# HGRN2 and retention heads: output matmuls behind the first eighth of the next head's first tile, back-transposes behind its seventh

## What is computed

```python
def _layer(x, c, pos, state, lb, g_norm, w_ada, b_ada, w_in, conv_w, conv_b, b_i, b_f, skip, w_gn, w_out):
    mod = jax.nn.silu(c) @ w_ada + b_ada
    shift, scale, gate = jnp.split(mod, 3, axis=-1)
    h = _rmsnorm(x, g_norm) * (1.0 + scale[:, None, :]) + shift[:, None, :]
    cols = jnp.split(h @ w_in, np.cumsum(COL_SIZES)[:-1].tolist(), axis=-1)
    hq, hf, hi, mq, mk, mv, mi, mf, rq, rk, rv, z = cols
    ...
    o = jnp.concatenate([
        _head_norm(o_hg, w_gn[:W_HG], False),
        _head_norm(o_ml, w_gn[W_HG:W_HG + W_ML], True) + skip * q_c.astype(jnp.float32),
        _head_norm(o_rt, w_gn[W_HG + W_ML:], True)], axis=-1)
    o = o.astype(x.dtype) * jax.nn.silu(z)
    y = x + gate[:, None, :] * (o @ w_out)
```

```python
        inter = inter_d[None, :, :, None] * jnp.einsum('bhtk,bhkv->bhtv', qc, s)
        sc = jnp.einsum('bhtk,bhsk->bhts', qc, kc) * intra_d[None]
        intra = jnp.einsum('bhts,bhsv->bhtv', sc, vc)
        s_new = (chunk_d[None, :, None, None] * s
                 + jnp.einsum('bhsk,bhsv->bhkv', kc * state_d[None, :, :, None], vc))
        return s_new, inter + intra
```

## Time and profile before

| what | us |
|---|---|
| median of 3 runs (2352.44 to 2353.47) | 2353.13 |
| span of the profiled execution | 2351.4 |
| TensorE matmuls busy, of this span | 2296.5 |
| VectorE busy | 1283.2 |
| ScalarE busy | 753.7 |
| GpSimd busy | 938.6 |

### The profile page before, as it was taken

One profiled execution on the slowest core, in us unless ns is written; L12 is line 12 of the kernel. 1 busy time (PEld: TensorE's weight loads), 2 busy tenths in 40 slices (PEclk: granted clock), 3 DMA queues, 4 the chain that ended last, 5 costly groups with the idle time before them and its releaser, 6 DMA issues.

```text
span 2351.4 us, 50350 instructions
## 1 busy us (share of the span) xinstructions
PE 2296.5 (98%) x21251; PEld 2174.7 (92%) x21251; DVE 1283.2 (55%) x2499; ACT 753.7 (32%) x1219; POOL 938.6 (40%) x668
## 2 busy tenths in 40 slices
PE   5899999999999999999999999999999999999998
PEld 3799999999999999998888999999999999999998
DVE  5465666677776333442127566567767744345444
ACT  2243332333333333421114333233333333334111
POOL 2143343444333444453333333343333344346552
PEclk8999999999999999999999999999999999999999
DMA  9972333555554434368887233355554434433443
GB/s 365 352 230 76 92 92 109 156 155 155 155 155 123 114 102 110 101 194 257 247 283 215 74 92 92 92 155 155 156 158 106 125 98 109 116 95 109 109 120 107
DMA packets 473482, 347.22 MB, mean 148 GB/s; under 512 B 18701, under 2 KB 417513, under 8 KB 471937
## 3 DMA queue, kind: packets, MB, share of 16 engines
q1 hardware_dynamic: 473258, 344.02, 49.9%
HBM read 312.07 MB, written 32.09 MB: 146 GB/s over the span
## 4 chain that ended last, share of the span: by engine, by line
PE 90%; DVE 4%; DMA 3%; DVEq 1%; issue 1%; ACT 1%; POOL 1%; SPq 0%; ACTq 0%; POOLq 0%
PE pj L722 72%; PE mx L728 3%; DMA rows<-in_w_ada 2%; PE mx L1087 2%; PE mx L1113 2%; PE mx L843 1%; PE mx L1101 1%; PE mx L809 1%; PE pj L1220 1%; PE mx L1065 1%; PE mx L1115 1%; PE mx L1105 1%; DVE t L1598 1%; PE mx L990 1%; DMA rows<-in_x_prompt 1%
## 5 line engine op out<-in xcount | busy, mean ns | idle before, releaser
L722 PE MATMUL pj<-hh,whi 128*128 128x260 f32 x4928 | 1419.9, 288 | 7.9 <-DVE hl L1598 7.6
L690 POOL TENSOR_TENSOR wlo<-raw,whi 128x512 fp32r<-128x512 f32 x632 | 893.0, 1444 | 1311.7 <-ACT whi L1302 1311.7
L722 PE MATMUL pj<-hl,whi 128*128 128x260 f32 x4928 | 1393.3, 283 | 0.0
L722 PE MATMUL pj<-hh,wlo 128*128 128x260 f32 x4928 | 1390.7, 282 | 0.0
L722 PEld LDWEIGHTS pj<-hh,whi 128*128 128x128 f32 x4928 | 929.4, 189 | 52.5 <-issue 47.1
L722 PEld LDWEIGHTS pj<-hl,whi 128*128 128x128 f32 x4928 | 929.1, 189 | 0.0
L722 PEld LDWEIGHTS pj<-hh,wlo 128*128 128x128 f32 x4928 | 928.6, 188 | 0.0
L1302 ACT ACTIVATE whi<-raw 128x2048 fp32r<-128x2048 f32 x158 | 302.9, 1919 | 252.0 <-PE pj L722 174.2
L1302 ACT ACTIVATE xv<-pj 128x260 f32<-128x260 f32 x188 | 64.7, 383 | 388.0 <-PE pj L722 387.8
L1598 DVE SCALAR_TENSOR_TENSOR o<-pj,mod,t 128x260 f32<-128x260 f32 (+1 forms) x56 | 24.6, 480 | 231.1 <-PE pj L722 215.5
L1302 ACT ACTIVATE t<-t 128x520 f32<-128x520 f32 (+1 forms) x125 | 78.9, 631 | 170.9 <-DVEq L1852 124.3
(11 more groups left out here) (304 smaller groups left out, 2329.8 us busy)
## 6 DMA issues: line engine op xcount, KB each, us to landing
raw<-in_w_in SPq DMA_DIRECT2D x256, 512.0 KB, 5.3
raw<-in_w_out SPq DMA_DIRECT2D x64, 512.0 KB, 5.5
lev<-in_w_ada SPq DMA_DIRECT2D x90, 256.0 KB, 4.9
rows<-in_w_ada SPq DMA_DIRECT2D x22, 1024.0 KB, 12.1
lev<-in_w_ada SPq DMA_DIRECT2D x39, 512.0 KB, 6.0
out<-ss SPq DMA_DIRECT2D x32, 512.0 KB
xv<-in_w_ada SPq DMA_DIRECT2D x25, 512.0 KB, 5.8
y_kept<-o SPq DMA_DIRECT2D x2, 4160.0 KB, 15.9
```

Of the source, the lines that this page charges most:

```text
L690: last = e.tensor_tensor((wlo_third if t == 2 else wlo[:, par, :])[:, cs], w[:, cs], high_of(t)[:, cs].bitcast(F32), ALU.subtract)
L722: last = e.matmul(pj[:, 2 * par + b, 0:HALF], w[:, par, kb * P:(kb + 1) * P], x[:, kb, b * HALF:(b + 1) * HALF], start=(kb == 0 and m == 0 ...
```

## The change

Two hook tables in `hooks_of`, and nothing else. HGRN2 heads (4 per layer) and retention heads other than the very first and the last of a layer (4 in the first layer, 5 in the second) get `outputs` behind part 0 of the next head's tile 0 and `back` behind part 6 of it. These are 17 places. The last head of each layer (h = 15) keeps its table, so do the mLSTM heads and the very first head.

```diff
                         if kind == "hg":
                             own = ({}, {2: (level_scores((-1, 0)),),
                                         **{lv + 2: (level_scores((lv,)),) for lv in range(1, 6)}},
-                                   {0: (level_scores((6,)),), 2: (rows,), 5: (states_u,), 7: (outputs,)})
-                            return own, {5: (back,)}
+                                   {0: (level_scores((6,)),), 2: (rows,), 5: (states_u,)})
+                            return own, {0: (outputs,), 6: (back,)}
...
-                        return ({}, {}, {1: (scores, rows), 5: (states_u,), 7: (outputs,)}), {5: (back,)}
+                        if h + 1 == NH:
+                            return ({}, {}, {1: (scores, rows), 5: (states_u,), 7: (outputs,)}), {5: (back,)}
+                        return ({}, {}, {1: (scores, rows), 5: (states_u,)}), {0: (outputs,), 6: (back,)}
```

## The result

The changed kernel takes 2358.89 us (median of 10 runs, 2356.79 to 2359.59) against 2352.84 us for the kernel before (10 runs, 2352.32 to 2356.22): a ratio of 1.0023 with a 95% interval of 1.0015 to 1.0031, slower by 0.23%. The prediction was 2349.4 us, faster by 0.16%, in a range of 2348.2 to 2351.9. It was wrong in sign and in size, by 9.5 us.

A forecast was written before the change was run, and what follows sets the result against it. TensorE was taken to bound the kernel, running through 90% of the span. Removing its waits at 17 places gains 3.7 us, all other terms 0: 2353.1 - 3.7 = 2349.4 us, range 2348.2 to 2351.9.

The forecast's parts named there:

- What bounds the kernel, and the wait that goes: TensorE bounds the span; its wait for VectorE's `ss` at L1113 goes, weight-load waits falling from 32 to 15.
- (b): At L1113 the switch has a larger step of its own, 0.21 us: gain 2.2 us, time 2350.9 us; chance 0.10.
- (c): At L1113 the 0.31 us step is the instruction's cost, not a wait: nothing gained, 2353.1 us; chance 0.05.
- The size of the gain: At 17 places the step from L722 to L1113 falls to 0.12 us: 5.78 us less 17 x 0.12, 3.74 us.
- the move itself: Instructions of `outputs` take 2.30 us at a tile's edge and inside a tile alike, so the place costs 0.
- rival (a): All of the weight loads' wait at `outputs` comes back: 0.26 us each, 4.4 us for 17 places, 2348.7 us; chance 0.09.
- The tile's wait: Next head's tile 0 needs its low weights 2.6 us sooner; GpSimd's slack hides this, cost 0.
- `back`: TensorE's wait for `ho` at `back` stays 0; VectorE's chain there becomes about 0.9 us shorter.
- Rival (d): At eight HGRN2 places VectorE's chain, held by GpSimd, makes `back` wait 1.33 us each: 2360.0 us; chance 0.04.
- What now runs later: `outputs` starts 1.28 us later against the tiles, as do VectorE's work, `back` and `head_done`; those waiting for them lose 0.
- VectorE goes on to the next head: Tightest case is head 5: its first convolution slips 0.3 us, absorbed by idle time before the next; cost 0.
- a later stretch: Sign of a wrong forecast: the mLSTM heads or the edge between layers take back what the 17 places give.

The follow-up runs named there:

- additions first: The changed kernel with the two 8-column additions of `gate_scans` ahead of its five scans: 2348.49 us against 2353.17 for the kernel before, ratio 0.9979.
- states earlier: The changed kernel, gate-scan additions ahead of the scans, `states_u` behind part 4 instead of 5 in ten mLSTM heads and each layer's last: 2352.42 us against 2352.77.
- `outputs` alone: The changed kernel with `back` behind part 5 again in all 17 places, only `outputs` moved: 2348.68 us against 2352.77 for the kernel before, ratio 0.9983.

## Why the prediction was wrong

**What bounds the kernel, and the wait that goes: right.** All 17 steps fell from at least 0.31 to 0.12 us, and the weight loads' waits for `ss` from 32 to 15, the number written down. Rivals (b) and (c) have fallen with that.

**The size of the gain: too small.** I had 3.74 us. The offset between the traces of additions first and of before, without the start-up and the edge between the layers, is 5.25 us over the 17 places. The term "the move itself" was put at 0, by the very first head, where `outputs` takes 2.30 us, as at the edge. In the moved places it takes 2.20 us. The very first head is a poor witness, because it waits too. It is one of the 32 in the earlier trace rows, and its step is 0.30 us like the others', with `ss` ending at 154.75:

```profile
154.53 0.28 PE L722 MATMUL pj<-hl,whi 128*128 128x260 f32 x1
...
153.53 1.22 DVE L1592 TENSOR_TENSOR ss<-ss,mx 128x1024 f32<-128x1024 f32 x1 [0.17 <-issue]
```

Behind a wait the second L1113 starts 0.21 us after the first, behind none 0.11, which is why the first four are busy for 0.71 us in the earlier trace rows and for 0.61 in the moved places. The mLSTM heads of the kernel states earlier show the same: in each of the ten whose `states_u` is moved, the 2.40 us of the kernel before became 2.30 as the step fell from 0.32 or 0.33 to 0.12. So the 0.10 us belongs to the wait and goes with it; why a wait delays the second matmul isn't shown. A place was worth 0.31 us on the average and not 0.22, more than rival (a) had too (0.26).

**The tile's wait: right.** No wait for `lo_done` came at the moved places.

**`back`: right, and by its mechanism.** The chain from `outputs` to `ho` shrank. The first two additions on `bag` in the changed kernel, against 1.92 us in the earlier trace rows:

```profile
221.35 0.92 DVE L1594 TENSOR_TENSOR bag<-bag 128x4 f32<-128x4 f32 x2
```

The margin at `back` in head 1 grew from 0.53 to 1.43 us (the last scaling ends at 225.07, L728 starts at 226.50), 0.90 us as predicted. Rival (d) has fallen at its place. Its mechanism, an operation of VectorE held for a whole subtraction, was the right one, one head further on.

**What now runs later: this is the step that failed.** The lateness of 1.28 us was right at `outputs`, and so was the entry of the list "VectorE goes on to the next head". I then looked for the tightest case by VectorE's idle time ahead of an operation, found head 5 with 1.14 us, and priced the step at 0. Head 2, which the prediction doesn't name, has 2.99 us of idle time ahead of its first large product, and is the safer one by that measure. But the time that matters there lies ahead of GpSimd: the additions ended 0.91 us ahead of its start, less than the 1.44 us by which they moved against it. (At `head_done` the lateness is 1.44 and not 1.28 us: it hangs on `back`, which is twelve projection matmuls later in the tile, 12 x 0.12 us, and not on the end of `outputs`.) The rule was in the text, and used on the `bag` additions where it brings a gain; it was not carried past `head_done`. The prediction had named a later stretch that takes back the gain as a sign of being wrong, but as one in the mLSTM heads or at the edge between the layers. This is one place in each layer, and it outweighs all 17.

**The price of a standstill.** Even with both waits of 3.3 us in hand I would have forecast 2352.8 - 5.25 + 2 x 3.47 = 2354.5 us. With the clock it is 2352.8 - 5.25 + 2 x 5.1 = 2357.8 us, 1.1 us below the median measured. The waits for gate loads, 0.8 to 1.1 us in each of both its profiles, may be the rest; that is not shown.

## What to carry to other kernels

Before anything is moved later, follow it through the next unit's first operations on the engine that takes it over, and ask of each how long before a colliding engine starts it ends; idle time ahead of the next operation doesn't answer that. Move what must be late and pin what others start from: `outputs` alone gave nearly the whole gain, and `back` brought all of the loss. Where VectorE's operations are held in GpSimd's time, get the short ones done ahead of it: 0.3 us of additions in the wrong place cost some 10 us.

## What the runs showed of the hardware

A standstill of TensorE of 3.25 us can cost half as much again and more. The granted clock fell to 0.50 at nine of ten such places, for about 3 us at six of them (4.84 to 4.95 us in all) and about 7 us at three (5.94 to 6.20), and at one it didn't (3.47). At four of the nine it fell in the last 1.1 us of the standstill and not behind it. With one of 2.13 us, in head 10 of the states-earlier kernel, it was down for 6 us and more. The Trainium skill, "TensorE: Matmul & The Clock Gate", section "What's actually happening", knows only these two levels, 1.2 and 2.4 GHz; the stretches shown, at 0.50 and 1.00, agree, and the 0.93 is a mean over both.

A small operation of VectorE that is held in GpSimd's time takes about one of GpSimd's subtractions, whatever its own size. Operations of 4 to 16 columns (0.13 to 0.21 us alone) and a copy of 128x256 (0.29 us) came out at 1.14 to 1.35 us, one behind the other. Not every operation there is held: the addition into `sw` took 0.51 us inside GpSimd's time in the earlier trace rows and 1.39 in the earlier trace rows.

The first matmuls behind a wait for a semaphore are slower in this kernel than the wait alone says: the first started 0.08 to 0.09 us behind VectorE, and the second 0.21 us behind the first instead of 0.11.
